# Expert pairs of a mixture-of-experts layer: 64 slots an expert on two column groups of the array, or 32 slots on four

## The reference

```python
g_idx = jnp.argmax(g_logits, axis=-1)                       # one of 4 groups
e_val, e_idx = lax.top_k(e_in_group, TOP_K_IN_GROUP)        # two of its 8 experts
...
a = jnp.einsum('nd,edh->neh', t, w_gate)                    # 32 experts, 1024 x 256
b = jnp.einsum('nd,edh->neh', t, w_up)
act = jax.nn.silu(a) * b * combine[:, :, None].astype(t.dtype)
out = jnp.einsum('neh,ehd->nd', act, w_down)                # 256 x 1024
```

## Time and profile before

| | |
|---|---|
| median of 3 runs | 1232.97 us (1231.89 to 1234.54) |
| the profiled execution | 1234.43 us, its span 1232.5 us |
| TensorE busy | 1086.0 us of the span (88%) |
| mean of the 16 DMA engines | 268 GB/s, 330.46 MB in all |
| the chain that ended last | PE 62%, DMA 22%, DVE 6% |

### The profile page before, as it was taken

How to read it: one execution, slowest core, us unless ns; L and a number is a source line. 1 busy time by engine, 2 the same in 40 slices (tenths; PEclk the granted TensorE clock), 3 DMA queues, 4 the chain that set the end, 5 groups by cost and what they waited for, 6 DMA issues and landing times.

```text
span 1232.5 us, 14744 instructions
## 1 busy us (share of the span) xinstructions
PE 1086.0 (88%) x5455; PEld 560.7 (45%) x5455; DVE 477.7 (39%) x1038; ACT 262.1 (21%) x514; POOL 187.8 (15%) x213
## 2 busy tenths in 40 slices
PE   5699978898899699999989999989988877888786
PEld 3344645554444243444445555647945322222224
DVE  2455667236132212332383335777362111111115
ACT  2211244213333021332341111000141011110104
POOL 1020000011332023221100001222013132111100
PEclk8999999999999799999999999999989989988989
DMA  9997895626699865999966020322281699999974
GB/s 349 387 334 291 246 337 209 273 74 230 236 399 403 351 246 204 396 396 401 381 233 229 1 102 1 117 122 96 110 329 50 248 413 412 414 414 408 412 318 153
DMA packets 95586, 330.46 MB, mean 268 GB/s; under 512 B 17547, under 2 KB 33323, under 8 KB 78725
## 3 DMA queue, kind: packets, MB, share of 16 engines
q1 hardware_dynamic: 71936, 303.49, 63.5%
q0 software_dynamic: 16848, 19.29, 4.7%
q10 hardware_dynamic: 6708, 6.45, 1.5%
HBM read 333.22 MB, written 35.35 MB: 299 GB/s over the span
## 4 chain that ended last, share of the span: by engine, by line
PE 62%; DMA 22%; DVE 6%; issue 3%; SPq 3%; ACT 2%; POOL 0%; ACTq 0%; POOLq 0%; DVEq 0%
PE bank L905 13%; PE bank L1073 10%; DMA ring<-in_moe_w_up 10%; PE bank L919 6%; PE bank L718 3%; PE bank L1115 3%; PE bank L834 3%; DMA hT<-in_hy_log_decay 3%; DMA ring<-in_w_ada 3%; PE bank L592 3%; PE bank L1104 2%; PE bank L627 2%; DMA ring<-in_moe_w_down 2%; PE bank L1059 2%; PE bank L610 1%
## 5 line engine op out<-in xcount | busy, mean ns | idle before, releaser
L905 PE MATMUL bank<-ring,work 128*64 128x512 f32 x1120 | 264.6, 628 | 41.0 <-DMA ring<-in_moe_w_up 30.5
L905 PEld LDWEIGHTS bank<-ring,work 128*64 128x64 f32 x1120 | 83.7, 144 | 211.3 <-issue 165.3
L919 PE MATMUL bank<-ring,work 128*64 128x512 f32 x560 | 132.3, 616 | 3.6 <-DVE work L1739 1.6
L1073 PE MATMUL bank<-hT,ring 128*128 128x384 f32 x384 | 126.3, 488 | 0.0
L1769 DVE SCALAR_TENSOR_TENSOR work<-bank,work 128x256 f32<-128x256 f32 x32 | 15.5, 484 | 251.9 <-ACT work L1313 231.3
L1073 PEld LDWEIGHTS bank<-hT,ring 128*128 128x128 f32 x384 | 72.2, 190 | 52.0 <-issue 2.3
L919 PEld LDWEIGHTS bank<-ring,work 128*64 128x64 f32 x560 | 38.1, 141 | 76.3 <-issue 66.4
L1786 DVE COPY work<-bank 128x512 f32<-128x512 f32 x32 | 22.1, 690 | 118.0 <-PE bank L919 97.7
L1313 ACT ACTIVATE work<-bank 128x256 f32<-128x256 f32 x32 | 12.2, 382 | 214.8 <-PE bank L905 213.8
L592 PE MATMUL bank<-ring,condS 128*32 128x256 f32 x768 | 47.3, 399 | 10.7 <-DVE ada L1433 5.5
L1938 POOL DMA_INDIRECT work<-token_vectors,work x28 | 28.7, 1024 | 164.6 <-PE bank L888 158.8
(11 more groups left out here) (306 smaller groups left out, 1507.9 us busy)
## 6 DMA issues: line engine op xcount, KB each, us to landing
ring<-in_moe_w_gate SPq DMA_DIRECT2D x32, 2048.0 KB
ring<-in_moe_w_up SPq DMA_DIRECT2D x32, 2048.0 KB
ring<-in_moe_w_down SPq DMA_DIRECT2D x32, 2048.0 KB, 22.7
ring<-in_w_ada SPq DMA_DIRECT2D x24, 2048.0 KB, 12.8
ring<-in_hy_w_in SPq DMA_DIRECT2D x6, 2048.0 KB, 15.4
expert_rows<-work POOLq DMA_DIRECT2D x6, 1024.0 KB, 15.4
filter_spectra<-work ACTq DMA_DIRECT2D x8, 768.0 KB
work<-expert_rows SPq DMA_DIRECT2D x16, 384.0 KB, 7.3
```

The costliest lines, as they stand in the source:

```text
L905: last = mm(bank[2][WIN * j:WIN * (j + 1), :], gt[:, k, WIN * j:WIN * (j + 1)], gu[:, :, j, k, :], start=(k == 0), stop=(k == KD - 1))
L919: last = mm(bank[b + hf][WIN * j:WIN * (j + 1), :], AT[:, k, WIN * j:WIN * (j + 1)], dn[:, j, k, hf * HALF:(hf + 1) * HALF], start=(k == 0 ...
L1073: last = mm(bank[n % 2][:, 0:T], w[:, k, (n % 4) * P:(n % 4 + 1) * P], hT[:, k, :], start=(k == 0), stop=(k == KD - 1))
```

## The change

A window has 32 slots an expert instead of 64. The 128 partitions that two experts no longer fill are used twice: partitions 0 to 63 hold one half of the columns and 64 to 127 the other. The inner 256 columns of an expert (gate and up) are split in halves over two 64-partition parts, and the 1024 output columns likewise, so `gate_up` and `down` run on four groups of 32 columns of the array with 256 streamed columns each. Token rows are moved as half rows of 2 KB: the gathers and scatters address rows of 512 columns, and `tab` holds the table twice, the second copy with its row numbers one higher. Inside `extra`, TensorE's waits for the weights and for `Y` move from ahead of the loop to the matmuls that need them.

```diff
-WIN = 64
+WIN = 32
+SLOTS = 2 * WIN
...
-                pool.dma_start(tab.rearrange("p (w q) -> p w q", w=NWIN),
-                               tabD[l].rearrange("(w p q) c -> p w (q c)", w=NWIN, p=P)).then_inc(S_("tab_in"), 16)
-                pool.wait_ge(S_("tab_in"), B_("tab_in") + 16)
+                for h in range(2):
+                    pool.dma_start(tab[SLOTS * h:SLOTS * (h + 1), :].rearrange("p (w q) -> p w q", w=NWIN),
+                                   tabD[l].rearrange("(w p q) c -> p w (q c)", w=NWIN, p=SLOTS)).then_inc(S_("tab_in"), 16)
+                pool.wait_ge(S_("tab_in"), B_("tab_in") + 32)
...
+                nc.gpsimd.tensor_tensor(places, places, half, ALU.add).then_inc(S_("g_clear"), 1)
...
-                    ind(out=G[:, q % 2, :], out_offset=None, in_=hD, in_offset=at_rows(tab[:, 4 * q + 1:4 * q + 2]),
+                    ind(out=G[:, q % 2, :], out_offset=None, in_=hH, in_offset=at_rows(tab[:, 4 * q + 1:4 * q + 2]),
...
                 def gather_turn(q, half):
-                    for kk in range(4):
-                        k = 4 * half + kk
-                        last = tr(bank[half][:, kk * P:(kk + 1) * P], G[:, q % 2, k * P:(k + 1) * P], ident)
+                    for i in range(2):
+                        b = 2 * half + i
+                        last = tr(bank[half][:, i * P:(i + 1) * P], G[:, q % 2, b * P:(b + 1) * P], ident)
...
                     for k in range(KD):
-                        for j in range(2):
-                            last = mm(bank[2][WIN * j:WIN * (j + 1), :], gt[:, k, WIN * j:WIN * (j + 1)], gu[:, :, j, k, :],
-                                      start=(k == 0), stop=(k == KD - 1))
+                        h, b = divmod(k, 4)
+                        for part in range(2):
+                            for j in range(2):
+                                at = SLOTS * part + WIN * j
+                                last = mm(bank[2][at:at + WIN, 0:2 * P], gt[:, b, SLOTS * h + WIN * j:SLOTS * h + WIN * (j + 1)],
+                                          gu[:, :, j, k, part * P:(part + 1) * P], start=(k == 0), stop=(k == KD - 1))
...
                         for k in range(2):
-                            for j in range(2):
-                                last = mm(bank[b + hf][WIN * j:WIN * (j + 1), :], AT[:, k, WIN * j:WIN * (j + 1)],
-                                          dn[:, j, k, hf * HALF:(hf + 1) * HALF], start=(k == 0), stop=(k == 1))
+                            for part in range(2):
+                                for j in range(2):
+                                    at, n0 = SLOTS * part + WIN * j, HALF * part + 256 * hf
+                                    last = mm(bank[b + hf][at:at + WIN, 0:256], AT[:, SLOTS * k + WIN * j:SLOTS * k + WIN * (j + 1)],
+                                              dn[:, j, k, n0:n0 + 256], start=(k == 0), stop=(k == 1))
...
                     with pe.If(hi > lo):
                         copied(q)
-                        pe.wait_ge(S_("y_set"), B_("y_set") + 2 * max(q, 1))
-                        pe.wait_ge(sem(f"gu_in_{s}"), B_("gu_in") + 32 * (q // 2 + 1))
-                        pe.wait_ge(sem(f"dn_in_{s}"), B_("dn_in") + 16 * (q // 2 + 1))
                         pe.wait_ge(S_("xnext_in"), 16 * (l * PAIRS + q + 1))
...
+                            pe.wait_ge(sem(f"gu_in_{s}"), B_("gu_in") + 32 * (q // 2 + 1))
                             gate_up(GTx, s, S_("xgu_mm"))
...
+                            pe.wait_ge(S_("y_set"), B_("y_set") + 2 * max(q, 1))
+                            pe.wait_ge(sem(f"dn_in_{s}"), B_("dn_in") + 16 * (q // 2 + 1))
                             down(s, 4, S_("xdn_mm"))
```

More of the change, by code:

```diff
@@ L144, in token_rows @@
     for k in range(2):
-        a[:, k, :, 0] = tok + k * T
-        a[:, k, :, 1] = tok
-    return a.reshape(P, TC * 8)
+        a[:, k, :, 0] = 2 * (tok + k * T)
+        a[:, k, :, 1] = 2 * tok
+        a[:, k, :, 3] = tok
+    half = np.tile(np.arange(P)[:, None] // SLOTS, (1, 2)).astype(np.int32)
+    return np.concatenate([a.reshape(P, TC * 8), half], 1)
 def build(nc, a):
@@ L465, in further @@
             return nc.s_assert_within(at, 0, top,
-                                      skip_runtime_bounds_check_because="a count is at most 384, so a window is at most 5")
+                                      skip_runtime_bounds_check_because="a count is at most 384, so a window is at most 11")
         def apart(eng):
@@ L876, in gather_mm @@
                 def gather_mm(q, half, blocks=(0, 1, 2, 3)):
-                    for kk in blocks:
-                        k = 4 * half + kk
+                    for i in blocks:
+                        b, h = 2 * half + i // 2, i % 2
                         for c in range(TC):
-                            last = mm(bank[half][:, kk * P:(kk + 1) * P], hTok[:, c, k * P:(k + 1) * P], onehot[:, q, c],
-                                      start=(c == 0), stop=(c == TC - 1))
+                            last = mm(bank[half][:, i * SLOTS:(i + 1) * SLOTS], hTok[:, c, (4 * h + b) * P:(4 * h + b + 1) * P],
+                                      onehot[:, q, c], start=(c == 0), stop=(c == TC - 1))
                     if blocks[-1] == 3:
@@ L903, in gate_up @@
                     for k in range(KD):
[L904 to L906 removed]
+                        h, b = divmod(k, 4)
[4 more added lines that the diff above has]
+                                          gu[:, :, j, k, part * P:(part + 1) * P], start=(k == 0), stop=(k == KD - 1))
                     last.then_inc(done, 1)
                 def turn_act(done):
[L910 to L912 removed]
+                    tr(bank[3][:, 0:P], A, ident).then_inc(done, 1)
                 def down(s, b, done):
@@ L936, in extra @@
                             pe.wait_ge(S_("xgath"), 16 * (x + 1))
-                            for k in range(KD):
-                                last = tr(turn_bank(q, k // 4)[:, k % 4 * P:(k % 4 + 1) * P], Gx[:, k * P:(k + 1) * P], ident)
+                            for b in range(4):
+                                last = tr(turn_bank(q, b // 2)[:, b % 2 * P:(b % 2 + 1) * P], Gx[:, b * P:(b + 1) * P], ident)
                             last.then_inc(S_("xgt_mm"), 1)
                             pe.wait_ge(S_("xgt_set"), 2 * (x + 1))
+                            pe.wait_ge(sem(f"gu_in_{s}"), B_("gu_in") + 32 * (q // 2 + 1))
                             gate_up(GTx, s, S_("xgu_mm"))
@@ L994, in last_rows @@
                 def last_rows(k):
-                    mm(bank[RES_BANK[k % 7]][:, 0:T], Y[:, 1, k * P:(k + 1) * P], rstd[:, :], start=True, stop=True)
+                    h, b = divmod(k, 4)
+                    own = slice(SLOTS * h, SLOTS * (h + 1))
+                    mm(bank[RES_BANK[k % 7]][:, 0:T], Y[own, 1, b * P:(b + 1) * P], rstd[own, :], start=True, stop=True)
                 def other_rows(k):
@@ L1970, in second @@
                     pool.wait_ge(S_("xnext"), l * PAIRS + q + 1)
[L1971 to L1972 removed]
+                    ind(out=Gx, out_offset=None, in_=hH, in_offset=at_rows(curx[:, 1:2]),
+                        bounds_check=2 * T - 1, oob_is_err=False).then_inc(S_("xnext_in"), 16)
                 if l == 0:
```

128 lines of the change are left out of this document (65 added, 63 removed).

## The result

The changed kernel takes 1362.68 us (median of 4 runs, 1356.6 to 1371.04), the kernel before 1233.37 us beside it: a ratio of 1.1051, 95% interval 1.1018 to 1.1084. It is 129 us slower. The profiled execution of after took 1356.6 us, the shortest of its four, with a span of 1354.6 us, so the difference of the two spans, which the traces can explain, is 1354.6 - 1232.5 = 122.1 us.

A forecast was written before the change was run, and what follows sets the result against it. Weights were taken to bound layer 1, weights and TensorE about equally layer 0, so silence of the weight queue counts. Layer 0 +28, layer 1 +76, tails -4: +100 us on 1234.4, 1.5 above the median, gives 1333; range 1275 to 1375.

The forecast's parts named there:

- main case: Whole kernel: +100 us, 1333 us, with its own range 1315 to 1355; chance 0.50.
- gate_up of 3.66 us: In a window, gate_up as 64 records on four column groups falls from 7.09 to 3.66 us, about 7 behind a wait.
- The rival in which four groups don't run side by side: Windows and pairs: gate_up stays 7.1 and down 3.65 us; some +85 more, 1418 us; chance 0.04.
- The rival of 2.4 GHz throughout: TensorE keeps its full clock, windows take 8.4 us; +52 instead of +100, 1285 us; chance 0.22.
- Layer 1: forecast +76: Late weight loads behind windows of pairs 0, 1, 2, 4, 6: 15.4, 26.0, 16.2, 9.0, 9.0 us, sum 76.
- the hop to the next pair: GpSimd's scatter and two gathers, from a window's end to the next pair's Gx: 27.4 us with weights streaming.
- Layer 0: forecast +28: Last loads end at 639 after silences in pairs 6, 7 and 9; last gate_up starts at 634 instead of 605.7.
- its window ends at 397.1 and the next loads at 401.2 are in time: Layer 0, pair 5: the moved wait and shorter window help, so its window delays no weight loads.
- pair 15's gate and up some 5 us sooner: its gate_up starts at 634: End of layer 0: gate and up land some 5 us before the last loads end at 639; gate_up 28 us later.
- Tails: End of each layer: last gate_up costs what it costs now (7.1 us), down saves 1.8; -2 us each.
- Longer hops: Gathers carry twice the valid rows; each hop under load takes the scatter's 9.46 us; +37, 1370 us; chance 0.14.
- The other side, faster by short hops: Hops under load take 2.5 us as in silence and the clock holds; -18, 1215 us; chance 0.07.

The follow-up runs named there:

- e3: The kernel before with further windows counted by 32 slots: thirteen windows of 64 slots, ten of them empty; 1439.6 us.
- e4: The changed kernel running only the three windows that a count by 64 gives, tokens of the other ten left out; 1233.68 us.
- e5: The changed kernel with ScalarE taking layer 0's decay factors in the odd pair, behind its Silu, not at the even pair's end; 1340.16 us.
- e2: The changed kernel with no further windows, tokens beyond the 32nd of an expert left out; 1211.79 us.
- e7: e2 with the matmuls that add the last pair's rows contracting over all 128 rows of Y instead of 64; 1181.82 us.
- the third edit: The edit of e7, last pair's rows summed over all 128 rows, here added to the edits of e5 and e6; 1295.21 us with all three.
- e8: The changed kernel with the edits of e5, e6 and e7 together, nothing left out; 1295.21 us.
- e6: The changed kernel with two buffers for a window's rows, the next pair's first window gathered before this pair's windows are handled; 1332.63 us.

## Why the prediction was right, and where it was off

Slower, and by the mechanism given: 1333 us forecast, 1362.7 measured, inside 1275 to 1375 but 8 us above the main case's own range. By its steps, on the profiled executions (forecast sum +100, measured +122.1):

- **Thirteen windows for three**: as forecast, pair by pair, and e3 and e4 show that their number is the loss.
- **gate_up of 3.66 us**: measured 3.66 where TensorE had just worked, and 4.5 to 6.8 behind waits, where 7 was forecast: the clock came back on the way. The rival in which four groups don't run side by side is out. A window behind a wait took 11.7 us in pair 1 of layer 1 (1052.44 to 1064.12), forecast 12.1. The rival of 2.4 GHz throughout is out as well: the granted clock was 0.73 to 0.83 in the stretches with windows.
- **Layer 1: forecast +76, measured +63.8** (last gate_up 1307.92 - 1194.66, less the 49.5 us with which the layer began late, 981.62 - 932.14). From the loads, at 16.4 us a pair, silences of 16.1, 20.5, 14.9, 7.9 and 5.5 us for 15.4, 26.0, 16.2, 9.0 and 9.0. The over-sized term is the hop to the next pair: 22.3 us (1030.11 to 1052.44) for 27.4. Its last gather took 3.2 us (1049.25 to 1052.44), the weights having landed by then, not the 7.87 of the earlier trace rows. Loads of pair 8 came 1178.50 - 1031.30 = 147.2 us after those of pair 2, for 158 forecast.
- **Layer 0: forecast +28, measured +53.7** (last gate_up at 659.43 against 605.69). Two steps failed. The first is "its window ends at 397.1 and the next loads at 401.2 are in time" for pair 5 and "is covered" for pair 13. TensorE was ready when I said, 385.94 for 385. I had followed the window through TensorE and GpSimd and not through ScalarE's queue, where its copy stands behind a wait for a load. The loads behind pair 5's window went out 12.4 us late by it (413.57 for 401.2), but two loads on they were near the forecast again (464.15 for 460.1, 513.33 for 512.1): from the end of pair 5's window to the rows of pair 6's it took 21.4 us and not 27.4, so two errors covered each other. Pair 13's wait was not covered: the last loads went out at 634.71, forecast 553.8 + 4 x 17.1 = 622.2. The second is "pair 15's gate and up some 5 us sooner: its gate_up starts at 634", which lets the weights end the layer. From the last loads to that gate_up it took 24.7 us for 11.8, and TensorE waited for no weights there: it was still at the rest of pair 13, at pair 14 and at the filters, with a stop of 4.3 us inside pair 14's gate_up. So of the gap of 25.7 us about 12.5 are late loads and 12.9 are TensorE's own lag, which I had let vanish. e5, with the first cause gone, brings 13 to 17 us by the traces and keeps the lag.
- **Tails: forecast -2 each, measured -4.3 and +8.8.** In layer 0 the last rows began at 2.4 GHz and stayed there (0.91 to 0.94 us a group). In layer 1 they fell to 1.2 GHz and stayed there. The last gate_up, forecast at 7.1, took 5.42. "down saves 1.8" was right and beside the point: I had put the 64-row matmuls at nothing, since they issue as many instructions as before. e2 and e7 put the clock at 15 us a layer where it falls, and the third edit still brings 14.9 us in e8.
- Together: 53.7 - 4.3 + 63.8 + 8.8, or 122.1 before rounding. The misses upward (25.7 in layer 0 and 10.8 in the last tail) outweigh those downward (12.2 in layer 1 and 2.3). That the sum came within 22 us is in part luck: the misses have different causes and opposite signs.
- **Longer hops** (rival, 1370): its time was near, its reason was not. Hops were shorter than forecast.
- **The other side, faster by short hops**: under load a scatter took 8.1 us and a gather 6.4 (1031.00 to 1039.06 and 1041.85 to 1048.28), far from the 2.5 in silence. The Trainium skill (DMA: Bandwidth & Descriptors, Anatomy of one DMA) would have 2.6 us for each by an estimate from its figures; the trace does not agree with it while weights stream, and it comes near only in silence.

## What to carry to other kernels

When a step comes ten times instead of three times, follow it through the queue of every engine that it touches, not only the slow one: here its copy on ScalarE stood behind an unrelated wait for a load, and that was a tenth to a sixth of the loss. A helper that issues one transfer and waits for it before the next has a throughput as well as a latency; where neighbouring steps all need it, taking away one wait moves the stall to a later one until the helper itself has less to do. And a smaller tile that needs more passes must be weighed by what stands between the passes (12.9 us a window or somewhat more, of which TensorE's gate_up and down at full clock are 5.6), not by what a pass computes.

## What the runs showed of the hardware

- A stretch of matmuls in which every other group contracts over 64 rows ran 25.3 us without a gap at a granted clock of 0.50 (e2, both layers). With all groups over 128 rows the clock fell as well, and came back (e7, 1.49 us a group and then 0.81). The Trainium skill (TensorE: Matmul & The Clock Gate, What's actually happening) says that the clock is throttled by default and that activity of the array releases it. The 128-row stretch agrees; in the 64-row stretch the engine was busy for 25.27 of 25.30 us and the clock stayed at its lower level, so the two stretches differ in a way that the sentence does not name. Where a 64-row stretch began at 2.4 GHz, it stayed there in layer 0 of after and of e5, where TensorE had stood still 0.57 and 0.60 us just before, and fell in layer 1 of after, e4 and e5 and in both layers of e6, where it had stood still 3.2 to 3.6 us. That the stop before it decides fits all seven; no run varied it alone.
- TensorE stood still inside gate_up, between matmuls of one group and with no wait to be seen, for 28.1 us in all in after (at most 5.3 us at once, put down to "issue"). In before the idle time of gate_up (41.0 us) has other causes: weights 30.5, VectorE 9.0, ScalarE 1.5, and e3, the old form with thirteen windows, has none of it either. The queue of instruction loads moved 1.31 MB against 0.95, and TensorE has 7986 records against 5455. That the engine waited for instructions is a guess; no run took it apart.
